# RWKV rounds: modulation sums without a total, a second key buffer, moved exponentials and rates, paired low rank products; a halved forward transform in the Hyena convolutions

## The chip, the cores and the metric

The kernel runs on one core of one Trainium2 chip. The metric is the time of the whole program on the device in microseconds (us). All data are 32-bit floats. Engines: PE is TensorE (matmuls; PEld its weight loads), DVE is VectorE, ACT is ScalarE, POOL is GpSimd, SP is SyncE, whose queue issues most transfers here.

## The reference, cut to what matters

A two-layer block works on 256 latent and 256 context tokens of width 1024. Layer 0 mixes tokens by a bidirectional RWKV-7 recurrence, layer 1 by an order-2 Hyena convolution (latent tokens alone); after each comes a mixture of 32 gated MLPs. The recurrence per head and direction is

```python
sa = jnp.einsum('zbhvk,zbhk->zbhv', S, a_t)
S = S * w_t[..., None, :] + sa[..., None] * b_t[..., None, :] + v_t[..., None] * k_t[..., None, :]
y = jnp.einsum('zbhvk,zbhk->zbhv', S, r_t)
```

with decay, rates and keys made from low rank products (`tanh(x @ w1) @ w2`, `(x @ a1) @ a2`), exponentials and a normalised key `kk`. The modulation rows `cond @ ada_w[i] + ada_b[i]` (6144 columns per layer) scale, shift and gate both layers. Hyena convolves with `irfft(rfft(u) * rfft(kern))`, twice in a row.

## The kernel before, in words

**Stages.** The inputs of the recurrence (to 70 us of the profile), the RWKV heads (71 to 720 us), the experts of layer 0 (from 725 us), the Hyena inputs (1221 to 1355 us), the Hyena convolutions (1356 to 1449 us), the experts of layer 1 (from 1450 us) and a final norm.

**The heads** (`rwkv_heads`) work on one block of 128 channels (two heads) a *round*, eight blocks in all. A round has 24 *slots*, three to a step of the chunked recurrence; here the three slots of a step are called a *hop*, hop 0 (slots 0 to 2) to hop 7 (slots 21 to 23). In round m, four blocks are in work: block m runs its recurrence (`chain`), block m+1 (`now`) has its products and triangular inverse made, block m+2 (`early`) has its projections made, and block m-1 (`behind`) is normalised. Rounds -2 and -1 fill this pipeline.

Each engine has a list of its own, written slot by slot, and runs it strictly in that order; semaphores tie the lists together. The chain of a hop is: PE `chain_state` (L918) → DVE `chain_state` (L1454 or L1456) → PE `chain_solve` (L937, L943) → ACT `chain_solve` (L1187) → PE `chain_close` (L951, L957) → DVE `chain_close` (L1469: the new state H) → next hop. All else is placed between as filler: PE's projections (L775), transposes `turn` (L794), the triangular inverse in levels (`level`, L886: z1, s1, s2, z2, x), products with the values (`from_values_early` L864, `from_values_late` L877, whose halves are called wy0 and wy1), and the feature products (L834 early half, L846 to L852 late half).

**Two rings of banks.** PSUM banks 0 and 1 are shared by all "open" uses in the order of `open_order()`: use i may start only when use i-2 has been read, by ACT or, for names `ys` and `h*`, by DVE. Three more banks serve the inverse in the same way (`inverse_order()`).

**Later modulation** (`LaterModulation`). While the heads run, the rows of `ada_w` that later stages need are multiplied: per round three pieces of 512, 384 and 384 columns, each in two halves (h0 to h5) of four row tiles. `products` (L239) puts the four tiles of a half side by side in four column groups of 32, 512 or 384 columns each; DVE's `modulate` adds the bank to an accumulator (L1490 first half, L1485 second); `total` (L246) sums the 128 partitions with a matmul by ones, ACT copies the row (L1194) and sends it to DRAM. SP loads the weights of h(k) when PE has finished h(k-1).

**Features of block m+1**, on DVE in slots 0 to 5: `key_rates` (L1310), `rates` (L1315), `key_products` (L1320), `features` (L1338 to L1340), `key_sum` (L1327), `features_kr` (L1346, L1348); ACT's `factors` (L1114 to L1118) gives their exponentials in slots 1 and 2. PE's early feature products stand in slot 6.

**Convolutions.** Per order (two) and half of the channels (two): PE transposes, a forward transform of 16 matmul passes (L2648), ACT copies of four banks (L2694), six DVE operations on the spectrum (L2705 to L2712), and 32 passes of the inverse transform (L2657).

## Time and profile before

| what | us |
|---|---|
| three timed runs | 1961.82, 1964.73, 1973.62 (median 1964.73) |
| the profiled execution, own time | 1960.14 |
| its span | 1958.2 |
| rounds 0 to 5 (147.9 to 588.2) | 440.3 |
| round 6, round 7 | 65.1, 52.7 |
| shortest rounds (3 and 4) | 72.0 each |

The page gives busy times over the whole span; since the stages have different limits, the windows by round and by hop say more. A window row has the length of the stretch, then for each engine its busy time and number of instructions, the granted TensorE clock (1.00 is 2.4 GHz, 0.50 is 1.2 GHz), the share of DMA time and GB/s. In a timeline row the bracket is the idle time of the engine before the instruction, and what ended it. A matmul of 32-bit floats shows as two passes.

### The profile page before, as it was taken

Reading aid. Unit: us, or ns where it says so; the run is one execution under the profiler, and the core shown is the slowest. Engines: PE = TensorE matmul, PEld = TensorE weight load, DVE = VectorE, ACT = ScalarE, POOL = GpSimd, SP = SyncE. Lnnn points to the kernel's source line nnn. Section 1 sums busy time; section 2 is a strip of 40 time slices with the busy share of each in tenths; the row PEclk is TensorE's granted clock in tenths of the full one; section 3 lists DMA queues with packets and bytes.
Section 4 is the critical chain, followed back from the end, with each engine's and each line's share of the span. In section 5 each row is a group of like instructions: output and inputs, shape, how many; then the busy total and the mean of one; then the engine's idle time right before and its main releaser. Section 6 shows DMA issues by size and latency. Waiting matters only on the chain. (4 is left out here: it accounts for less than half of the span.)

```text
span 1958.2 us, 34257 instructions
## 1 busy us (share of the span) xinstructions
PE 1776.7 (91%) x13979; PEld 941.9 (48%) x13979; DVE 773.4 (39%) x1910; ACT 531.2 (27%) x993; POOL 52.1 (3%) x45
## 2 busy tenths in 40 slices
PE   5788898898897888999999999898999999999996
PEld 2344555555555544443443443675654444444442
DVE  5766677777777335200100101564735110110101
ACT  3244454554454321111111111213321111111111
POOL 0010000000100000000000001000000000000001
PEclk8989899999999899999999999999999999999998
DMA  9013323323323468999999997232166999999993
GB/s 308 26 33 101 99 73 114 114 77 111 110 76 127 162 238 360 427 428 428 428 429 428 428 416 277 76 128 112 82 272 272 427 428 428 428 428 428 428 413 123
DMA packets 105168, 504.05 MB, mean 257 GB/s; under 512 B 15568, under 2 KB 60352, under 8 KB 79184
## 3 DMA queue, kind: packets, MB, share of 16 engines
q1 hardware_dynamic: 103728, 501.88, 64.4%
q8 instruction: 91, 1.49, 0.3%
q10 hardware_dynamic: 1312, 0.37, 0.1%
q14 instruction: 37, 0.30, 0.0%
HBM read 501.13 MB, written 1.09 MB: 256 GB/s over the span
## 5 line engine op out<-in xcount | busy, mean ns | idle before, releaser
L2009 DVE TENSOR_TENSOR arena<-banks,arena 128x512 f32<-128x512 f32 x32 | 22.1, 692 | 660.5 <-PE banks L1821 660.5
L1821 PE MATMUL banks<-arena 128*64 128x512 f32 x1024 | 226.4, 594 | 10.5 <-DMA arena<-in_moe_w_up 10.5
L1843 PE MATMUL banks<-arena 128*64 128x512 f32 x1024 | 226.8, 596 | 3.3 <-ACT arena L1940 3.3
L1812 PE MATMUL banks<-arena 128*64 128x512 f32 x1024 | 225.3, 593 | 3.3 <-DVE arena L1932 3.3
L775 PE MATMUL banks<-arena 128*128 128x512 f32 (+1 forms) x384 | 159.3, 553 | 0.8 <-ACT arena L1086 0.8
L1821 PEld LDWEIGHTS banks<-arena 128*64 128x64 f32 x1024 | 82.1, 137 | 152.8 <-issue 152.8
L1812 PEld LDWEIGHTS banks<-arena 128*64 128x64 f32 x1024 | 74.2, 137 | 147.8 <-issue 144.2
L1843 PEld LDWEIGHTS banks<-arena 128*64 128x64 f32 x1024 | 70.7, 137 | 154.4 <-issue 150.7
L1934 ACT ACTIVATE arena<-banks,arena 128x128 f32<-128x128 f32 x128 | 48.1, 456 | 335.5 <-PE banks L1801 335.5
L1801 PEld LDWEIGHTS banks<-arena 128*128 128x128 f32 x1024 | 118.4, 194 | 28.1 <-issue 24.3
L1801 PE MATMUL banks<-arena 128*128 128x128 f32 x1024 | 124.5, 281 | 3.5 <-DVE arena L2004 3.5
L1850 PE MATMUL banks<-arena 128*128 128x512 f32 x256 | 115.4, 594 | 2.4 <-ACT arena L1945 2.4
L775 PEld LDWEIGHTS banks<-arena 128*128 128x128 f32 x384 | 69.9, 195 | 59.1 <-issue 50.6
L1944 ACT ACTIVATE arena<-banks 128x512 f32<-128x512 f32 x32 | 19.1, 597 | 282.6 <-PE banks L1843 282.6
L2428 PE MATMUL banks<-arena 128*128 128x256 f32 x384 | 88.9, 391 | 0.0
L2428 PEld LDWEIGHTS banks<-arena 128*128 128x128 f32 x384 | 74.5, 196 | 18.1 <-issue 7.0
L1932 DVE TENSOR_SCALAR arena<-banks,arena 128x128 f32<-128x128 f32 x128 | 43.7, 404 | 97.1 <-PE banks L1801 97.1
L1850 PEld LDWEIGHTS banks<-arena 128*128 128x128 f32 x256 | 46.2, 191 | 50.0 <-issue 45.9
L239 PE MATMUL banks<-arena 128*32 128x384 f32 (+1 forms) x384 | 49.3, 587 | 21.2 <-DMA arena<-in_ada_w 14.1
L1925 ACT ACTIVATE arena<-banks 128x512 f32<-128x512 f32 x32 | 19.1, 597 | 169.7 <-PE banks L1812 169.7
L1187 ACT ACTIVATE arena<-banks 128x128 f32<-128x128 f32 x64 | 17.9, 279 | 133.4 <-PE banks L937 133.4
L918 PE MATMUL banks<-arena 64*64 64x64 f32 x512 | 24.4, 245 | 25.0 <-DVEq L1470 25.0
(394 smaller groups left out, 2398.0 us busy)
## 6 DMA issues: line engine op xcount, KB each, us to landing
arena<-in_moe_w_gate SPq DMA_DIRECT2D x64, 2048.0 KB, 14.9
arena<-in_moe_w_up SPq DMA_DIRECT2D x64, 2048.0 KB, 17.1
arena<-in_moe_w_down SPq DMA_DIRECT2D x64, 2048.0 KB, 12.8
arena<-in_ada_w SPq DMA_DIRECT2D x128, 192.0 KB, 2.9
arena<-in_ada_w SPq DMA_DIRECT2D x64, 256.0 KB, 3.5
arena<-in_rw_wrkv SPq DMA_DIRECT2D x24, 512.0 KB, 5.1
arena<-in_hy_w_in SPq DMA_DIRECT2D x6, 2048.0 KB, 8.4
arena<-in_ada_w SPq DMA_DIRECT2D x8, 1024.0 KB, 17.0
```

The costliest lines, as they stand in the source:

```text
L239: mm = pe.matmul(bank[g * 32:(g + 1) * 32, 0:self.width(piece)], self.cond[:, half * self.HALF + g], self.w[g][:, 0:self.width(piece)], st ...
L775: mm = pe.matmul(s.psum[OPEN.bank(n, name)][:, 0:width], wkv[k][:, t], x[:, t], start=(t == 0), stop=(t == KT - 1))
L918: mm = pe.matmul(s.psum[5 + h][rows(z), 0:C], a_of(par, z, j)[rows(h)], H[rows(h), z], start=True, stop=True)
L1801: mm = pe.matmul((X0, X1)[k // 4][:, k % 4 * P:(k % 4 + 1) * P], hx[:, t, k * P:(k + 1) * P], sel[par][:, t].rearrange("p a b -> p (a b)") ...
L1812: mm = pe.matmul(G[j * CAP:(j + 1) * CAP, :], xT[:, t, j * CAP:(j + 1) * CAP], wg[par][j][:, t], start=(t == 0), stop=(t == KT - 1))
L1821: mm = pe.matmul(U[j * CAP:(j + 1) * CAP, :], xT[:, t, j * CAP:(j + 1) * CAP], wu[j][:, t], start=(t == 0), stop=(t == KT - 1))
L1843: mm = pe.matmul(bank[j * CAP:(j + 1) * CAP, :], hT[:, t, j * CAP:(j + 1) * CAP], wd[j][:, t, half * 512:(half + 1) * 512], start=(t == 0) ...
L1850: pe.matmul(OUT[k][:, :], selwT[par][:, k // 2], y[:, k % 2 * 512:(k % 2 + 1) * 512], start=start, stop=stop).then_inc(scat_done, 1)
L1932: op = eng.tensor_scalar(xT[:, k], src, sc[:, k:k + 1], sh[:, k:k + 1], ALU.mult, ALU.add)
L1934: op = eng.activation(xT[:, k], src, ACT.Identity, bias=sh[:, k:k + 1], scale=sc[:, k:k + 1])
L2009: dve.tensor_tensor(h, U[:, :], sg, ALU.mult).then_inc(h_ready, 1)
L2428: mm = pe.matmul(s.psum[n % 2][:, 0:L], win_ring[k][:, t, q * P:(q + 1) * P], hT[:, t], start=(t == 0), stop=(t == KT - 1))
```

## The change

1. **No totals.** A modulation product now splits its 512 (384) columns over the four column groups, 128 (96) each, and accumulates the four row tiles in the bank: 16 matmuls of 128 (96) columns in place of 4 of 512 (384). DVE adds bias and halves on 128 (96) columns; `total` on PE and on ACT is gone; SP stores the row, in `store`, ahead of the next piece's bias load. The accumulator, bias and row buffers shrink from 512 to 128 columns.
2. **Second key buffer** `KK`; `key_rates`, `key_products` and `rates` of a block move a round ahead, to slots 20, 22 and 23; `inner_factors` (both directions) to slot 21 and `outer_factors(0)` to slot 22 on ACT, `outer_factors(1)` stays in slot 1.
3. **Slots.** Early feature products from slot 6 to 5, h0 from 3 to 2 ahead of wy0, h1 from 6 to 7, `level_two_z` from 7 to 6, `from_values_early` ahead of h3, the decay pair w from 13 to 14 behind h3, the rate pair a behind h4. SP's `load_first` from slot 2 to 4, h1's load from 4 to 3.
4. **Pairs.** `low_rank` takes both banks and issues its two matmuls one after the other; `sum_directions` interleaves its two row halves. ACT evaluates one sigmoid of a constant in slot 11.
5. **Convolutions.** The forward transform multiplies the even and the odd tokens apart (8 passes, no accumulation), and DVE makes the two frequency halves as sum and difference, four operations more; ACT copies the two even banks.

```diff
-        self.acc, self.bias, self.row = s.take(512), s.take(512), s.take(512)
+        self.acc, self.bias, self.row = s.take(P), s.take(P), s.take(P)
...
+    def store(self, sp, m, piece, open_dve):
+        layer, cols = self.place(m, piece)
+        sp.wait_ge(open_dve, OPEN.taken(m, f"h{2 * piece + 1}")[1])
+        sp.dma_start(self.mods[layer, 0, cols].rearrange("(g n) -> g n", g=4),
+                     self.row[0:P:32, 0:self.part(piece)]).then_inc(self.row_out, 16)
...
-        for g in range(self.HALF):
-            mm = pe.matmul(bank[g * 32:(g + 1) * 32, 0:self.width(piece)], self.cond[:, half * self.HALF + g],
-                           self.w[g][:, 0:self.width(piece)], start=True, stop=True, tile_position=(0, g * 32))
+        n = self.part(piece)
+        for t in range(self.HALF):
+            for g in range(4):
+                mm = pe.matmul(bank[g * 32:(g + 1) * 32, 0:n], self.cond[:, half * self.HALF + t],
+                               self.w[t][:, g * n:(g + 1) * n], start=(t == 0), stop=(t == self.HALF - 1), tile_position=(0, g * 32))
...
-        order += [(m, u) for u in ("wy0", "wy1", "h0") if chain]
-        order += [(m, u) for u in ("h1", "t0") if chain]
+        order += [(m, u) for u in ("h0", "wy0", "wy1") if chain]
+        order += [(m, u) for u in ("h1",) if chain]
...
-    BB, KK = [s.take(STEPS, 2, C) for _ in range(2)], s.take(STEPS, 2, C)
+    BB, KK = [s.take(STEPS, 2, C) for _ in range(2)], [s.take(STEPS, 2, C) for _ in range(2)]
...
+                banks = [open_bank(n, f"{name}{z}") for z in range(2)]
+                for z in range(2):
+                    pe.matmul(banks[z][:, :], w[rows(z), :], x[rows(z), :], start=True, stop=True).then_inc(open_done, 1)
...
-                    if now and slot == 1:
-                        factors(n, 0)
...
+                    if early and slot == 21:
+                        inner_factors(q, 0)
+                        inner_factors(q, 1)
+                    if early and slot == 22:
+                        outer_factors(q, 0)
...
-                    if now and slot == 0:
-                        key_rates(n)
+                        features_a(n, 0)
...
                     if early and slot == 20:
                         key_norms(q, 0)
+                        key_rates(q)
...
+                    if early and slot == 22:
+                        key_products(q)
                     if early and slot == 23:
                         unit_keys(q)
+                        rates(q)
...
                         for i in range(TT):
-                            mm = pe.matmul(s.psum[4 + n][:, :], fwd[part][:, i, ft * P:(ft + 1) * P],
-                                           vt[:, i, half * 512:(half + 1) * 512], start=(i == 0), stop=(i == TT - 1))
-                        mm.then_inc(dft_done, 1)
+                            pe.matmul(s.psum[4 + part * 2 + i][:, :], fwd[part][:, i, 0:P],
+                                      vt[:, i, half * 512:(half + 1) * 512], start=True, stop=True).then_inc(dft_done, 1)
...
+                        a, b = half_even[part], s.psum[5 + part * 2][:, :]
+                        dve.tensor_tensor(vhat[:, part, 0, c], a, b, ALU.add)
+                        first, second = ((a, b), (b, a))[part]
+                        dve.tensor_tensor(vhat[:, part, 1, c], first, second, ALU.subtract).then_inc(vhat_ready, 1)
```

How the lists move, at three places. In the rows, "x16" counts equal instructions in a row; the line numbers of the changed kernel differ by a few.

**PE, hop 0's end to the start of hop 2**, before: L886 (64x64 x16) is a level, L877 wy0 and wy1, L918 state, L239 a modulation product, L834 the early feature products.

```order
L886 MATMUL banks<-arena 64x64 x16
L877 MATMUL banks<-arena 64x64 x16
L918 MATMUL banks<-arena 64x64 x4
L877 MATMUL banks<-arena 64x64 x16
L239 MATMUL banks<-arena 32x512 x4
L937 MATMUL banks<-arena 64x64 x4
L943 MATMUL banks<-arena 64x64 x4
L886 MATMUL banks<-x_res,arena 64x64 x16
L886 MATMUL banks<-arena,x_res 64x64 x16
L951 MATMUL banks<-arena 64x64 x4
L918 MATMUL banks<-arena 64x64 x4
```

The same place in the changed kernel (L893 level, L884 wy, L925 state, L253 modulation product, L841 early feature products):

```order
L893 MATMUL banks<-arena 64x64 x16
L253 MATMUL banks<-arena 32x128 x16
L884 MATMUL banks<-arena 64x64 x16
L925 MATMUL banks<-arena 64x64 x4
L884 MATMUL banks<-arena 64x64 x16
L944 MATMUL banks<-arena 64x64 x4
L950 MATMUL banks<-arena 64x64 x4
L893 MATMUL banks<-x_res,arena 64x64 x16
L893 MATMUL banks<-arena,x_res 64x64 x16
L958 MATMUL banks<-arena 64x64 x4
L841 MATMUL banks<-arena 64x64 x32
L925 MATMUL banks<-arena 64x64 x4
```

The product h0 now stands between the level and wy0, and the early feature products between the close of hop 1 and the state of hop 2.

**PE, hop 4's second half and the start of hop 5**, before: L820 ends the rows of block m-1, L766 is the pair w, L951 and L957 close hop 4, L239 is h3, L864 the early values, L918 and L922 the state of hop 5, L246 a total, L775 the key projection.

```order
L820 MATMUL banks<-const,arena 128x128 x2
L766 MATMUL banks<-arena 128x512 x2
L951 MATMUL banks<-arena 64x64 x4
L957 MATMUL banks<-arena 64x64 x4
L239 MATMUL banks<-arena 32x384 x4
L864 MATMUL banks<-arena 64x64 x16
L918 MATMUL banks<-arena 64x64 x4
L922 MATMUL banks<-arena 64x64 x4
L246 MATMUL banks<-arena,const 1x384
L775 MATMUL banks<-arena 128x512 x2
```

Now (L827, L958 and L964, L871, L253, L776, L925 and L929, L785 in the same roles):

```order
L827 MATMUL banks<-const,arena 128x128 x2
L958 MATMUL banks<-arena 64x64 x4
L964 MATMUL banks<-arena 64x64 x4
L871 MATMUL banks<-arena 64x64 x16
L253 MATMUL banks<-arena 32x96 x16
L776 MATMUL banks<-arena 128x512 x2
L925 MATMUL banks<-arena 64x64 x4
L929 MATMUL banks<-arena 64x64 x4
L785 MATMUL banks<-arena 128x512 x2
```

The pair w has moved behind h3 and stands directly ahead of hop 5's state; the total is gone.

**DVE, the end of hop 7 and the start of the next round**, before: L1449 adds the identity to z2, L1475 is the output sum, L1303 the unit keys, L1454 and L1458 the state of hop 0, then key rates (L1310), rates (L1315) and key products (L1320).

```order
L1449 TENSOR_TENSOR x_res<-banks,const 128x512
L1475 TENSOR_TENSOR arena<-banks,arena 128x128
L1303 SCALAR_TENSOR_TENSOR arena<-arena 128x512
L1454 TENSOR_TENSOR arena<-banks,arena 128x2x64
L1458 TENSOR_TENSOR arena<-arena 128x128
L1310 TENSOR_SCALAR arena<-arena 128x1024
L1315 TENSOR_TENSOR arena<-arena 128x8x64
L1315 TENSOR_TENSOR arena<-arena 128x2x4x64
L1320 TENSOR_TENSOR arena<-arena 128x8x64
L1320 TENSOR_TENSOR arena<-arena 128x2x4x64
```

Now (L1446, L1314 key products, L1472, L1296 unit keys, L1308 rates, L1451 and L1455 the state, L1332 the first feature):

```order
L1446 TENSOR_TENSOR x_res<-banks,const 128x512
L1314 TENSOR_TENSOR arena<-arena 128x8x64
L1314 TENSOR_TENSOR arena<-arena 128x2x4x64
L1472 TENSOR_TENSOR arena<-banks,arena 128x128
L1296 SCALAR_TENSOR_TENSOR arena<-arena 128x512
L1308 TENSOR_TENSOR arena<-arena 128x8x64
L1308 TENSOR_TENSOR arena<-arena 128x2x4x64
L1451 TENSOR_TENSOR arena<-banks,arena 128x2x64
L1455 TENSOR_TENSOR arena<-arena 128x128
L1332 SCALAR_TENSOR_TENSOR arena<-arena 128x256
```

The key products and rates now stand ahead of hop 0's state, for the next block but one of the chain; the key rates have moved before these rows, between the two halves of the key norms.

## Rows read from the trace of the kernel before

**Rows 1.** The page: GB/s moved, in 40 slices of 49 us.
```profile
GB/s 308 26 33 101 99 73 114 114 77 111 110 76 127 162 238 360 427 428 428 428 429 428 428 416 277 76 128 112 82 272 272 427 428 428 428 428 428 428 413 123
```

**Rows 2.** Windows: rounds 0 to 5 together, round 6, round 7; columns named first.
```profile
core 0: us, PE busy (x) PEld busy (x) DVE busy (x) ACT busy (x) POOL busy (x), PEclk, DMA share, GB/s
147.90:588.20 440.30, 383.89 (x6133) 237.53 (x6128) 314.32 (x769) 214.75 (x387) 30.09 (x24) 0.97 0.33 98
588.20:653.30 65.10, 51.43 (x979) 34.63 (x978) 42.24 (x110) 28.49 (x54) 4.97 (x4) 0.87 0.42 141
653.30:706.00 52.70, 48.54 (x656) 26.05 (x656) 17.65 (x53) 9.50 (x23) 0.04 (x1) 0.97 0.37 121
```

**Rows 3.** Windows, same columns: the eight hops of round 3.
```profile
370.90:377.90 7.00, 5.55 (x120) 4.78 (x121) 5.29 (x12) 6.11 (x13) 0.00 (x0) 1.00 0.66 175
377.90:385.90 8.00, 4.96 (x151) 3.85 (x147) 6.16 (x15) 3.35 (x7) 0.00 (x0) 1.00 0.41 133
385.90:395.10 9.20, 7.88 (x246) 5.79 (x248) 7.63 (x20) 0.86 (x2) 2.51 (x2) 1.00 0.30 89
395.10:404.50 9.40, 9.40 (x71) 3.91 (x66) 5.93 (x19) 4.15 (x7) 0.00 (x0) 1.00 0.01 3
404.50:413.70 9.20, 7.32 (x115) 4.74 (x111) 7.79 (x20) 5.94 (x11) 0.00 (x0) 1.00 0.49 145
413.70:424.10 10.40, 9.67 (x70) 4.12 (x70) 8.99 (x22) 8.25 (x15) 0.00 (x0) 1.00 0.23 76
424.10:432.00 7.90, 7.90 (x155) 4.91 (x156) 4.41 (x14) 5.29 (x8) 0.00 (x0) 1.00 0.26 80
432.00:442.90 10.90, 9.92 (x138) 6.72 (x133) 6.77 (x9) 2.15 (x6) 2.50 (x2) 1.00 0.36 122
```

**Rows 4.** Timeline of PE, round 3: start, us, line, operation, count, idle before.
```profile
377.10 1.05 PE L877 MATMUL banks<-arena 64*64 64x64 f32 x29 [1.45 <-ACT arena L1081]
...
385.88 0.35 PE L918 MATMUL banks<-arena 64*64 64x64 f32 x8 [2.90 <-DVEq L1470]
...
387.28 1.16 PE L834 MATMUL banks<-arena 64*64 64x64 f32 x64
...
414.87 0.81 PE L246 MATMUL banks<-arena,const 128*1 128x384 f32 x2 [0.73 <-DVE arena L1485]
```

**Rows 5.** Timeline of PEld: the weight loads of one modulation product (eight passes).
```profile
379.43 0.16 PEld L239 LDWEIGHTS banks<-arena 128*32 128x32 f32 x8 [0.27 <-ACT arena L1140]
```

**Rows 6.** Groups of PE: busy us, mean ns, idle before and its releasers.
```profile
L239 PE MATMUL banks<-arena 128*32 128x384 f32 (+1 forms) x384 | 49.3, 587 | 21.2 <-DMA arena<-in_ada_w 14.1 <-ACT arena L1086 6.2
...
L246 PE MATMUL banks<-arena,const 128*1 128x384 f32 (+1 forms) x48 | 22.0, 539 | 4.3 <-DVE arena L1485 4.3
```

**Rows 7.** Timeline of DVE, round 3.
```profile
373.28 1.29 DVE L1315 TENSOR_TENSOR arena<-arena 128x512 f32<-128x512 f32 x2
...
378.82 0.68 DVE L1449 TENSOR_TENSOR x_res<-banks,const 128x512 f32<-128x512 f32 x1
...
394.58 0.28 DVE L1373 TENSOR_TENSOR arena<-banks,const 128x128 f32<-128x128 f32 x1
...
401.96 0.48 DVE L1469 SCALAR_TENSOR_TENSOR arena<-banks,arena 128x64 f32<-128x64 f32 x2 [1.81 <-PE banks L951]
...
413.13 0.47 DVE L1469 SCALAR_TENSOR_TENSOR arena<-banks,arena 128x64 f32<-128x64 f32 x2 [0.18 <-issue]
```

**Rows 8.** Timeline of PE before round 0: the first low rank pair.
```profile
72.80 1.13 PE L766 MATMUL banks<-arena 64*128 64x512 f32 x4 [3.07 <-DVEq L1537]
```

**Rows 9.** Windows, same columns: the stretch right after the same wait in round 0.
```profile
163.00:166.30 3.30, 2.92 (x48) 1.24 (x48) 1.95 (x5) 0.00 (x0) 0.00 (x0) 0.50 0.00 0
```

**Rows 10.** Timeline of the convolutions, PE and DVE.
```profile
1374.97 13.98 PE L2657 MATMUL banks<-arena 128*128 128x256 f32 x64
...
1399.36 7.13 PE L2648 MATMUL banks<-arena 128*128 128x512 f32 x16 [0.79 <-ACT arena L2690]
...
1368.14 1.22 DVE L2706 TENSOR_TENSOR arena<-arena 128x1024 f32<-128x1024 f32 x1
```

More of the change, by code:

```diff
@@ L226, in load @@
             sp.wait_ge(open_done, OPEN.done(*before))
-            if half == 0:
-                sp.wait_ge(open_dve, OPEN.taken(*before)[1])
         if half == 0:
-            sp.dma_start(self.bias[0:1, 0:self.width(piece)], self.ins["ada_b"][layer, cols].unsqueeze(0)).then_inc(self.bias_in, 16)
+            if m or k:
+                self.store(sp, *((m, piece - 1) if piece else (m - 1, self.PIECES - 1)), open_dve)
+            sp.dma_start(self.bias[0:P:32, 0:self.part(piece)],
+                         self.ins["ada_b"][layer, cols].rearrange("(g n) -> g n", g=4)).then_inc(self.bias_in, 16)
         for g in range(self.HALF):
@@ L541, in open_order @@
         order += [(m + 2, u) for u in ("rg",) if early]
-        order += [(m, u) for u in ("t2",) if chain]
     return order
@@ L620, in rwkv_heads @@
     wide = S1b
+    spare = s.take(1)
     later = LaterModulation(s, ins, mods)
@@ L703, in _ @@
                 for slot in range(SLOTS):
-                    if slot == 2 and 0 <= n and n + 1 < CH:
+                    if slot == 4 and 0 <= n and n + 1 < CH:
                         sp.wait_ge(open_done, OPEN.done(n, "rg"))
@@ L807, in sum_directions @@
                 pe.wait_ge(y_ready, HALF * (n + 1))
-                for c in range(HALF):
-                    out = bank[rows(c % 2), c // 2 * P:(c // 2 + 1) * P]
-                    pe.matmul(out, s.c("ident")[:, 0:C], Y[:, c], start=True, stop=False)
-                    mm = pe.matmul(out, s.c("ident")[:, C:P], Y[:, HALF - 1 - c], start=False, stop=True)
+                for pair in range(HALF // 2):
+                    out = [bank[rows(c), pair * P:(pair + 1) * P] for c in range(2)]
+                    for c in range(2):
+                        pe.matmul(out[c], s.c("ident")[:, 0:C], Y[:, 2 * pair + c], start=True, stop=False)
+                    for c in range(2):
+                        mm = pe.matmul(out[c], s.c("ident")[:, C:P], Y[:, HALF - 1 - 2 * pair - c], start=False, stop=True)
                 mm.then_inc(open_done, 1)
@@ L1037, in _ @@
                         modulate(m, 4)
+                    if early and slot == 18:
+                        low_rank(q, "a")
                     if early and slot == 19:
@@ L1054, in _ @@
                         level_two(n, 0)
-                    if chain and slot == 23:
-                        total(m, 2)
                     if m == CH - 1 and slot >= 9:
@@ L1187, in chain_solve @@
                 act.activation(U, s.psum[7][:, 0:P], ACT.Copy).then_inc(us_ready, 1)
-            def total(m, piece):
-                width = later.width(piece)
-                bank = read(m, f"t{piece}")
-                if m or piece:
-                    act.wait_ge(later.row_out, 16 * (later.PIECES * m + piece))
-                act.activation(later.row[0:1, 0:width], bank[0:1, 0:width], ACT.Copy).then_inc(open_act, 1)
-                act.wait_ge(open_act, OPEN.taken(m, f"t{piece}")[1])
-                layer, cols = later.place(m, piece)
-                act.dma_start(mods[layer, 0, cols].unsqueeze(0), later.row[0:1, 0:width]).then_inc(later.row_out, 16)
             for m in ROUNDS:
@@ L1230, in _ @@
                         values(n)
+                    if early and slot == 11:
+                        act.activation(spare, s.c("ones")[:, 0:1], ACT.Sigmoid)
                     if now and slot == 12:
@@ L1237, in _ @@
                         act.activation(outT, read(m - 1, "rows")[:, :], ACT.Copy).then_inc(open_act, 1)
-                    if early and slot == 13:
-                        decay_rank(q, 0)
-                        decay_rank(q, 1)
                     if now and slot == 14:
@@ L1243, in _ @@
                         spread(n)
-                    if chain and slot == 15:
-                        total(m, 1)
+                    if early and slot == 14:
+                        decay_rank(q, 0)
+                        decay_rank(q, 1)
                     if now and slot == 16:
@@ L1261, in _ @@
                         level_two(n, 0)
-                    if chain and slot == 23:
-                        total(m, 2)
-            act.wait_ge(later.row_out, CH * later.PIECES * 16)
         @block.vector
@@ L1574, in _ @@
                         row_scales(m - 1)
-                    if now and slot == 7:
+                    if now and slot == 6:
                         kept_early(n)
@@ L1594, in _ @@
                         modulate(m, 3)
-                    if early and slot == 14:
-                        decay_sum(q, 0)
                     if now and slot == 15:
                         turn_out(n)
+                    if early and slot == 15:
+                        decay_sum(q, 0)
                     if early and slot == 16:
@@ L2614, in hyena_layer @@
         ("vT_done", "vt_ready", "dft_done", "vhat_ready", "real_ready", "imag_ready", "y_done", "y_ready"))
-    o_done, skip_ready = S("o_done"), S("skip_ready")
+    o_done, skip_ready, half_ready = S("o_done"), S("skip_ready"), S("half_ready")
+    half_even = [half_b[:, part] for part in range(2)]
     with nc.Block(name="hyena_convolutions", no_gpsimd_drain=True) as block:
```

148 lines of the change are left out of this document (70 added, 78 removed).

## The prediction

> **What bounds the kernel now.** I first read the page's rate of transfers: about 428 GB/s, level, through the slices of both expert stages [rows 1]. Those stages take weights as fast as they come, and their loads are started by the end of the heads and of the convolutions; so what is won before them shifts them along whole, and only the heads and the convolutions have to be costed. The windows by round come next: rounds 0 to 5 take 440.3 us, 73.4 on average, with PE busy 383.9 of it and DVE 314.3 [rows 2]. PE is nearly the bound, but not quite: in round 3, a round of 72.0 us at full clock throughout, the hops show which engine it is [rows 3]. Hops 3 and 6 are all PE (9.40 of 9.40, 7.90 of 7.90). In hops 1, 2 and 4 PE is idle for 1.3 to 3.0 us. The timeline names the waits: 1.45 us for ACT's transposed values, held up behind the exponentials, and 2.90 us for DVE, which has all features ahead of the new state [rows 4]. In hop 4 it is DVE: from the state of hop 3 (401.96) to that of hop 4 (413.13) it works without a pause of over 0.5 us, 11.2 us, and PE's next state waits for it [rows 7]. So a round alternates between three bounds, and an edit is worth what it does in its own hop.
>
> **The change, hop by hop of round 3.** Prices: 24 totals are busy 22.0 us, 0.92 each, and wait 4.3 us in all for DVE; 48 modulation products take 49.3, 1.03 each [rows 6].
>
> *The new product* is not in the trace. Its 32 passes stream the same number of columns per column group as its 8 passes do now. Sixty-four quadrant passes of 64 columns take 1.16 us [rows 4], so short passes do run abreast. Bounds: 0.8 us (384 columns now) and, if the four groups ran one after another, 32 passes at a quarter of a 512-column pass (7.13 / 16 = 0.446 us [rows 10]), 3.6 us. I take 1.03, unchanged, since the short passes of [rows 4] are the nearest. The weight loads must overlap for that, and now they do: eight loads fall within 0.16 us, under a product still in flight [rows 5].
>
> The Trainium skill, "TensorE: Matmul & The Clock Gate", section "Part 3: Packing small matmuls", says that weight loads overlap matmuls in flight only when the row group differs. All passes of a product share one row group, so by that rule 32 passes would alternate with 32 loads, which is the slow rival below. The eight loads of [rows 5] contradict it, at least for loads to different column groups.
>
> *Hop 0 (7.0):* h0 moves in, 5.55 busy + 1.03 = 6.6, and ACT's hold-up goes, since only one direction's outer exponentials are left between the turned values. wy0's bank now waits for DVE's row means, which come late in the hop: about 0.4. 7.0, no change.
>
> *Hop 1 (8.0):* h0 and the 2.90 us go. A new wait comes: wy1 takes the bank of h0, which DVE reads after its state step and the identity add (0.68 [rows 7]); with the product's add at 128 columns (0.28, as L1373 [rows 7]) and the starts of the two state operations some 0.4, about 1.5 us in which PE has nothing else, since its list is strict. The early feature products (1.0) move in behind the close and need the features, which are now half done by then. 4.96 busy - 1.03 + 1.0 + 1.5 + 0.4 of handing over = 6.8: **-1.2**.
>
> *Hop 2 (9.2):* 7.88 busy - 1.0 (early products) - 0.92 (total) = 6.0; waits for DVE's masking of the banks stay, 0.8: 6.8, **-2.4**.
>
> *Hop 3 (9.4):* all projection: no change.
>
> *Hop 4 (9.2):* here it gets longer. DVE's list is the bound and keeps its length but for one narrower add (0.56 to 0.28), while the pair w, formerly ahead of the close, now stands behind h3 and takes h3's bank. So PE waits for DVE's state (0.47), output sum and product add, about 1.3 us from 413.13 on, then runs the pair (1.13 [rows 8]), and only then hop 5's state, which today starts 0.6 us after 413.13. 1.3 + 1.1 - 0.6 = 1.8, less 0.2 for the add: **+1.6**. Queued behind this wait are the next state and the key projection; PE idles some 2.7 us.
>
> *Hop 5 (10.4):* total and its wait go (0.85 + 0.73 [rows 4]); the key projection waits about 0.3 for ACT's sigmoid, now behind the spread: **-1.2**.
>
> *Hop 6 (7.9):* the pair a waits for h4's add on DVE (0.45) and the norm for the first rate (0.4), less what running side by side saves: **+0.4**.
>
> *Hop 7 (10.9):* the total (0.85) and the wait for weights (9.92 busy of 10.9, part of 14.1 us of such waits over all products [rows 6]) go, as h4 ends earlier; PE waits 0.2 for DVE's state, now behind the key rates: **-1.2**. DVE takes up key rates, products and rates here, 3.4 us (each pair 1.29 [rows 7]); its 4.1 us of idle time in this hop (6.77 busy of 10.9 [rows 3]) covers it. Without that cover the next round's first state would come up to 3.4 us late.
>
> *SP and the rest, at nothing:* the row stores stand ahead of bias and weight loads and wait for DVE's add. For h0 that add comes in the middle of hop 7, some 9 us ahead of the product; for h2 and h4 12 us. h1's weights now precede `load_first`, which is wanted in slot 14. The constant's sigmoid only moves a table load of ACT ahead of the bc and kc copies; the value projection's last part covers it.
>
> Sum: -1.2 - 2.4 + 1.6 - 1.2 + 0.4 - 1.2 = -4.0 per round, 72.0 to 68.0. The six rounds hold 440.3 - 6 × 72.0 = 8.3 us more than six short ones. Most of it is lower clock: right behind the 2.90 us wait the granted clock is 0.50 in round 0 [rows 9], though 1.00 in round 3. The new wait of 2.7 us in hop 4 is of that size, so I keep the 8.3 and count 6 × 4.0 = **24 us**. Round 6 has no block in `early`, so no pair and no +1.6; hops 1 and 2 (3.6), two more totals (1.8) and their waits (0.6): **6 us** of its 65.1. Round 7 has neither features nor pairs: three totals, **2.7 us**.
>
> *Convolutions.* The forward transform falls from 7.13 us to half, four times: 14.3 us of PE's work [rows 10]. DVE gets four operations on a bank per half, 0.68 each as the add of the same shape in [rows 7], beside six of 1.22 [rows 10] and their drains: 11 us a half. DVE then bounds both halves: one order is 1.04 + 0.74 + 1.8 (transposes, copy, first two banks) + 22 + 3.5 (a quarter of the 13.98 us inverse) = 29.1 us, against 1.04 + 0.74 + 7.13 + 1.04 + 0.79 + 7.13 + 13.98 = 31.9 now. Two orders: **5.7 us**, between nothing and 14.3.
>
> In all 24 + 6 + 2.7 + 5.7 = 38.4, so 1960.1 becomes 1921.7. That is the profiled execution; the median of the timed runs lies 4.6 above it and the fastest 1.7. I forecast **1924** for the new median, 2.1% below 1964.7. About 1% (19.6 us) is what a measurement of this kernel tells from no change.
>
> **The rivals.**
>
> A, the forecast: 1910 to 1938 as single terms vary, chance 0.52.
>
> B, *DVE's lists take over*. PE now meets DVE at wy1 and at the pair w in every round. If both waits come out 0.5 longer, and the clock is at its lower level for 3.3 us behind each hop 4 (1.65 us lost), 4.0 becomes 1.3 per round: 8 + 4 + 2.7 + 3 = 18 us, 1944. For it: DVE is busy 53 of 72 us and idles little in hops 4 and 5. Against: hop 5 has slack on PE. Chance 0.24.
>
> C, *more than counted*: lower clock gone and the wait in hop 4 half covered, 6.5 us per round: 39 + 6 + 2.7 + 5.7 = 53, 1909. Chance 0.14.
>
> D, *slower*: the narrow passes don't run abreast. A product then costs 3.6 in place of 1.03 at 128 columns and 1.9 more at 96; a round 2 × 2.5 + 4 × 1.9 = 12.6 us more, eight rounds 101: 2025. It decides from 1.2 us a product on (38 + 20 over 48). [Rows 4] and [rows 5] speak against it. Chance 0.04.
>
> E, *the edits don't bite*: the pairs run one after the other (+0.9 each, 11 us in six rounds) and the convolutions are held by DVE at today's length (5.7): 1941. [Rows 8] shows a pair abreast when both banks are free. Chance 0.06.
>
> **How the numbers follow.** The time is A's. Below 1945 lie A, C, most of E and half of B: faster 0.82; same, the rest of B and E, 0.13; slower, D and a little of the unforeseen, 0.05. The range 1906 to 1946 leaves out D, the upper end of B and the lower of C, 0.18 in all.
>
> **What would show it.** Windows by hop should show hops 1 and 2 at about 6.8 each, hop 4 near 10.8 with an idle time of PE of about 2.7 ended by DVE's add ahead of the pair, no wait of the state of hop 2, and a product group still near 1.03 us each. A product at 2 us or more makes D; a hop 5 at lower clock in most rounds makes B. The convolutions should take 88 us with PE waiting for DVE in the inverse. Hop 4 no longer than now would make the +1.6 wrong; rounds above 71 us, the whole ledger.

## The result and the profile after

On one chip, in alternation, the kernel before took 1965.83 us and the changed one 1946.5 (medians of seven runs each): a ratio of 0.9902, 95% interval [0.9879, 0.9925]. The kernel became faster by 1%, not by the forecast 2.1%. The profiled executions differ by less than the medians: the span falls from 1958.2 to 1944.6, 13.6 us where the ledger has 38.4.

Windows of the changed kernel for rounds 0 to 5, round 6 and the part of round 7 that answers to [rows 2]; columns: stretch, length, busy time (instructions) of each engine, granted clock, DMA share, GB/s.

```profile
core 0: us, PE busy (x) PEld busy (x) DVE busy (x) ACT busy (x) POOL busy (x), PEclk, DMA share, GB/s
153.60:583.30 429.70, 368.18 (x6958) 256.11 (x6956) 307.37 (x770) 206.10 (x375) 30.03 (x24) 0.95 0.33 99
583.30:645.90 62.60, 46.64 (x1122) 37.51 (x1119) 38.47 (x108) 23.78 (x45) 4.00 (x4) 0.89 0.45 147
645.90:695.70 49.80, 44.98 (x806) 28.08 (x802) 15.82 (x53) 7.96 (x19) 1.04 (x1) 1.00 0.43 139
```

Six rounds win 10.6 us, not 24. PE has 15.7 us less to be busy with than in [rows 2], at a mean clock of 0.95 (0.97 before). Round 6 wins 2.5 (forecast 6), round 7 2.9 (2.7). And the chain starts 5.7 us later, at 153.6 in place of 147.9: the fill rounds, for which the ledger has no term. These four make 10.3 us; the other 3.3 are won behind the heads, 2.1 of them in the two orders of the convolutions (64.4 to 62.4). The expert stages are level at 428 GB/s as in [rows 1], so all that is won ahead of them counts.

The eight hops of round 4, which is typical (72.0 us), in the same columns; they answer to [rows 3].

```profile
439.20:447.00 7.80, 6.65 (x162) 5.63 (x158) 6.27 (x16) 3.59 (x8) 0.00 (x0) 1.00 0.35 109
447.00:454.80 7.80, 6.19 (x202) 6.05 (x200) 4.07 (x11) 2.56 (x5) 0.00 (x0) 0.78 0.93 286
454.80:463.10 8.30, 5.94 (x221) 5.35 (x212) 5.14 (x15) 0.28 (x1) 2.51 (x2) 1.00 0.17 46
463.10:472.60 9.50, 9.50 (x93) 4.50 (x89) 7.01 (x24) 4.19 (x7) 0.00 (x0) 1.00 0.19 55
472.60:483.80 11.20, 6.99 (x138) 4.97 (x134) 7.95 (x21) 7.25 (x14) 0.00 (x0) 0.98 0.39 119
483.80:494.10 10.30, 10.17 (x65) 4.63 (x64) 8.24 (x20) 6.74 (x11) 0.00 (x0) 0.86 0.25 77
494.10:502.00 7.90, 7.02 (x182) 5.13 (x183) 4.60 (x15) 5.09 (x8) 0.00 (x0) 1.00 0.33 104
502.00:511.30 9.30, 8.98 (x158) 6.93 (x156) 8.65 (x11) 5.00 (x10) 2.49 (x2) 1.00 0.16 49
```

Hops 3, 6 and 7 are within 0.1 of the forecast or better. Hops 1 and 5 have a granted clock of 0.78 and 0.86: each holds a stretch at 0.50, and the clock column says where the time went before any wait is looked at. PE's waits in the same round, the longest ones (total, times, longest):

```profile
PE banks L776 <- DVE arena L1484: 3.5, 1, 3.5
PE banks L884 <- DVE arena L1487: 1.6, 1, 1.6
PE banks L893 <- issue: 1.5, 1, 1.5
PE banks L853 <- DVE arena L1370: 0.8, 1, 0.8
PE banks L944 <- DVE arena L1451: 0.7, 1, 0.7
```

The first two are the waits that the forecast introduced: the pair w (L776) behind DVE's add of h3, 3.5 where 2.7 was reckoned, and wy1 (L884) behind the add of h0, 1.6 where 1.5 was. The third has no releaser: PE pauses in the middle of a level whose first passes have run. Nothing like it stands in rounds 0 to 5 before; here there are 7.2 us of it in six rounds. Right behind the two waits, two windows:

```profile
449.20:452.60 3.40, 3.40 (x70) 3.40 (x72) 2.03 (x5) 0.77 (x2) 0.00 (x0) 0.50 0.93 289
483.30:486.70 3.40, 3.27 (x21) 1.56 (x20) 2.02 (x5) 1.27 (x2) 0.00 (x0) 0.50 0.51 150
```

Both are full of work, as in [rows 9], at half the clock (the 1.2 GHz level). Stretches of this kind hold 44.4 us of rounds 0 to 5, 23.9 before; at the pair w one begins in each of the six rounds (in two of them up to 0.9 us before the wait ends), behind wy1 in five.

Why the pair waits so long stands in DVE's list (timeline; start, us, line, operation, idle before):

```profile
477.00 1.03 DVE L1425 TENSOR_TENSOR x_res<-arena 128x512 f32<-128x512 f32 x1
478.11 0.69 DVE L1427 TENSOR_REDUCE arena<-x_res 128x64 f32<-128x512 f32 x1
478.87 1.07 DVE L1431 TENSOR_TENSOR x_res<-arena 128x512 f32<-128x512 f32 x1
480.01 0.69 DVE L1433 TENSOR_REDUCE arena<-x_res 128x64 f32<-128x512 f32 x1
480.88 0.48 DVE L1466 SCALAR_TENSOR_TENSOR arena<-banks,arena 128x64 f32<-128x64 f32 x2 [0.19 <-issue]
481.48 0.29 DVE L1472 TENSOR_TENSOR arena<-banks,arena 128x128 f32<-128x128 f32 x1
482.11 0.26 DVE L1484 TENSOR_TENSOR arena<-banks,arena 128x96 f32<-128x96 f32 x1 [0.34 <-issue]
```

PE ended h3 at 478.99. DVE is in the largest step of its triangular solve until 480.70, and only then come the close and the add (L1484) that frees the bank.

The products themselves, all rounds; 1536 rows of the new kind:

```profile
L253 PE MATMUL banks<-arena 128*32 128x96 f32 (+1 forms) x1536 | 46.5, 260 | 8.8 <-DMA arena<-in_ada_w 7.1
```

46.5 / 48 = 0.97 each, in place of 1.03 in [rows 6], with 7.1 us of waits for weights in place of 14.1. The rows of PE in the convolutions' two orders:

```profile
1347.10 5.26 PE L2646 MATMUL banks<-arena 128*128 128x512 f32 x8 [0.69 <-ACT arena L2687]
...
1368.27 10.07 PE L2654 MATMUL banks<-arena 128*128 128x256 f32 x32 [3.25 <-DVE arena L2713]
...
1385.27 3.70 PE L2646 MATMUL banks<-arena 128*128 128x512 f32 x8 [0.74 <-ACT arena L2687]
1388.87 7.45 PE L2654 MATMUL banks<-arena 128*128 128x256 f32 x32
1399.56 7.45 PE L2654 MATMUL banks<-arena 128*128 128x256 f32 x32 [3.24 <-DVE arena L2713]
```

The transform takes 3.70 where it took 7.13 [rows 10], and DVE then holds the inverse up by 3.24. The second order, at full clock, lasts 28.7 us (1378.18 to 1406.85); before it was 31.4. In the first order the same rows take 5.26 and 10.07, at half clock for part of them: 33.7.

### The profile page after: what moved, and what is told of

It is laid out like the page before. It is cut to its first block and busy times, and to the rows that moved or that the text cites. A ratio compares the mean times of both kernels' runs of the same rounds, so it can differ in the third digit from the quotient of the medians.

```text
span 1944.6 us, 36382 instructions
## 1 busy us (share of the span) xinstructions
PE 1745.5 (90%) x15051; PEld 963.6 (50%) x15051; DVE 772.1 (40%) x1926; ACT 515.4 (27%) x969; POOL 52.1 (3%) x45
## 5 line engine op out<-in xcount | busy, mean ns | idle before, releaser
L785 PE MATMUL banks<-arena 128*128 128x512 f32 (+1 forms) x384 | 166.4, 572 | 2.7 <-ACT arena L1086 2.4
L785 PEld LDWEIGHTS banks<-arena 128*128 128x128 f32 x384 | 72.4, 202 | 60.9 <-issue 47.3
L253 PE MATMUL banks<-arena 128*32 128x96 f32 (+1 forms) x1536 | 46.5, 260 | 8.8 <-DMA arena<-in_ada_w 7.1
L1466 DVE SCALAR_TENSOR_TENSOR arena<-banks,arena 128x64 f32<-128x64 f32 x112 | 26.8, 280 | 65.1 <-PE banks L958 61.9
L776 PE MATMUL banks<-arena 64*128 64x512 f32 x64 | 22.5, 777 | 27.0 <-DVE arena L1484 18.6
## 6 DMA issues: line engine op xcount, KB each, us to landing
arena<-in_moe_w_up SPq DMA_DIRECT2D x64, 2048.0 KB, 17.1
```

The lines of the kernel that those rows point to most:

```text
L253: mm = pe.matmul(bank[g * 32:(g + 1) * 32, 0:n], self.cond[:, half * self.HALF + t], self.w[t][:, g * n:(g + 1) * n], start=(t == 0), stop ...
L776: pe.matmul(banks[z][:, :], w[rows(z), :], x[rows(z), :], start=True, stop=True).then_inc(open_done, 1)
L785: mm = pe.matmul(s.psum[OPEN.bank(n, name)][:, 0:width], wkv[k][:, t], x[:, t], start=(t == 0), stop=(t == KT - 1))
L1466: dve.scalar_tensor_tensor(H[:, z], s.psum[5 + z][:, 2 * C:3 * C], fade[m % 2][:, z, j:j + 1], Hf[:, z], ALU.mult, ALU.add)
```

## The experiments

Ratios are to the kernel before, in runs on the same chip; 0.001 is 2 us. Variants are compared with one another by these ratios. Figures for rounds and hops come from one profiled execution of each; two executions with unchanged heads (before, and the convolutions alone) take 440.3 and 441.3 for rounds 0 to 5.

### One wait away at a time

The pair w back ahead of the close (lists of PE and ACT, and the ring of banks):

```diff
+                    if early and slot == 13:
+                        low_rank(q, "w")
...
-                    if early and slot == 14:
-                        low_rank(q, "w")
```

> The changed kernel with the pair w back where it was, ahead of the close of hop 4 and of h3 (ACT's sigmoids of it ahead of its spread, as before). Theory CLOCK: the 3.5 us wait and the low clock behind it go; hops 4 and 5 together fall from 21.5 to about 18.5 where PE stays fed, fill rounds get about 3 us shorter: about 1926. Theory WAITS: DVE's state is what hop 5 waits for whichever way, so hop 4 stays at 10.3 or more, PE waits about 2.5 us for the state in place of the pair, and the low clock stays behind that: 1938 to 1944, most of the gain in the fill rounds.

0.9803, [0.9783, 0.9823]; median 1929.14. Windows for rounds 0 to 5 and for hops 4 and 5 of round 4:

```profile
154.60:568.10 413.50, 360.20 (x6964) 254.69 (x6961) 306.79 (x770) 205.91 (x375) 30.02 (x24) 0.97 0.35 103
464.70:473.50 8.80, 7.02 (x136) 5.02 (x132) 7.41 (x19) 6.53 (x13) 0.00 (x0) 1.00 0.49 151
473.50:482.40 8.90, 8.88 (x68) 4.01 (x68) 7.29 (x20) 7.43 (x13) 0.00 (x0) 1.00 0.28 90
```

21.5 us have become 17.7, and the clock is 1.00: the wait for DVE's close is now covered by the pair, and no stretch at 0.50 stands at hop 4 in any round. This is CLOCK's picture; only the fill rounds did not get shorter (first state at 154.6). Over the six rounds hops 4 and 5 win 4.2 us on average, of which hops 2 and 6 give back 1.6; the pauses without a releaser grow from 7.2 to 10.2 us in all.

h0 behind wy1 again:

```diff
-        order += [(m, u) for u in ("h0", "wy0", "wy1") if chain]
+        order += [(m, u) for u in ("wy0", "wy1", "h0") if chain]
```

> The changed kernel with h0 back behind wy0 and wy1, so that wy1 no longer takes the bank that DVE reads late. Theory CLOCK: the wait of 1.6 us and the low clock in hop 1 go; hops 0 to 2 fall from 23.4 to about 20.5 in rounds 1 to 6: 1946.5 - 6 x 2.7 = about 1930. Theory WAITS: DVE's features set the early products, and PE waits in hop 1 or 2 for those; hops 0 to 2 stay above 22.5: 1941 to 1947.

0.9832, [0.9816, 0.9848]; median 1932.75. Hops 0 to 2 of round 4:

```profile
430.40:436.50 6.10, 5.40 (x130) 4.71 (x128) 5.58 (x14) 3.59 (x8) 0.00 (x0) 1.00 0.33 107
436.50:443.20 6.70, 6.04 (x236) 5.50 (x235) 4.72 (x14) 2.67 (x5) 0.00 (x0) 1.00 0.35 101
443.20:450.60 7.40, 5.74 (x219) 5.33 (x210) 5.17 (x15) 0.28 (x1) 2.52 (x2) 1.00 0.80 228
```

23.9 has become 20.2, with no stretch at 0.50 in hop 1, while those behind the pair w stay. So in these runs each wait keeps its own low stretches: taking one away leaves those of the other. Rounds 0 to 5 take 415.4. Not all of that is wait and clock: the pauses without a releaser nearly go too, 1.6 us in the six rounds in place of 7.2.

Both together:

> The changed kernel with both: the pair w ahead of the close of hop 4 and h0 behind wy1. Alone they took 17.4 and 13.8 us off 1946.5 (rounds 0 to 5: 413.5 and 415.4 in place of 429.7). If the two waits are independent, as the forecast's ledger by hops has it: rounds 0 to 5 near 400, 1946.5 - 31 = about 1915. If DVE's list is the next bound (it is busy about 53 us of a round), PE waits for DVE elsewhere and less than 24 of the 31 come: above 1922.

0.9754, [0.9731, 0.9778]; median 1917.35. Below the changed kernel (0.9902) that is 9.9 and 7.0 thousandths alone and 14.8 together, 29 us of a sum of 33: the waits are nearly independent.

### The wait kept, the clock kept up

Multiplications of the identity, whose result nobody reads, in front of the two waiting operations:

```diff
+                        s.keep_warm(pe, inverse_bank(m, "s1l"), 3)
                         from_values_late(m, 1)
...
+                            s.keep_warm(pe, inverse_bank(n, "z1c"), 7)
                         low_rank(q, "w")
```

> The changed kernel (1946.5) with TensorE kept busy in its two new waits: three multiplications of the identity with constants (512 columns, 0.43 us each as the four at the end of the convolutions) ahead of wy1, seven ahead of the pair w, into a bank that the inverse takes next. The waits for DVE stay as long as they are. Theory CLOCK (the clock that falls to 0.50 behind these waits costs most of what is missing; rounds 0 to 5 hold 44 us of such stretches, 20 before, on 42 us of PE work): the stretches behind the two waits go, hops 1 and 5 get about 1.5 shorter each, rounds 0 to 5 fall from 429.7 to about 414, the kernel to about 1930. Theory WAITS (DVE's list sets the end of hops 1, 2, 4 and 5, and a faster PE only waits longer): the stretches go but rounds 0 to 5 stay above 425 and the kernel above 1941.

0.9952, [0.9934, 0.997], slower than the changed kernel: neither theory's number. The amount was wrong. The timeline of PE in hop 4 of round 4:

```profile
486.90 6.28 PE L94 MATMUL banks<-const 128*128 128x512 f32 x14
493.11 1.13 PE L776 MATMUL banks<-arena 64*128 64x512 f32 x4
```

Seven multiplications are 14 passes and end 4 us after the bank was free. With one and three of them:

> The changed kernel with TensorE kept busy in its two new waits, by the right amount this time: a multiplication of 512 columns is two passes of 0.43, 0.87 us (14 rows in 6.3 us in the run with seven), so one ahead of wy1 (wait 1.6) and three ahead of the pair w (2.6 of 3.1 to 3.6 us). Theory CLOCK: the stretches at 0.50 behind both waits go and nothing else gets longer; hop 5 falls from 10.6 to 9.4 and hop 1 by 0.5 as in the run with too much work, rounds 0 to 5 from 429.7 to about 418, the kernel to about 1934. Theory WAITS: no gain, 1943 or more.

0.987, [0.9849, 0.9891]; median 1936.65. Rounds 0 to 5 take 423.0 in place of 429.7, and 17.1 us of them are at 0.50 in place of 44.4, all behind pauses (below), none behind the two waits. The clock alone, with the waits as they were, is worth 6.7 us there and about 6 in the ratio. The two intervals overlap, so the timed runs alone do not settle it; the windows speak for it, and the run with few passes below, which fills the waits in the same way, takes 420.6. Hops 1 and 5 of round 5 (9.4, with a pause of 1.4 in it, and 10.1 in the changed kernel):

```profile
513.20:519.40 6.20, 5.64 (x204) 4.75 (x201) 4.06 (x11) 2.56 (x5) 0.00 (x0) 1.00 0.90 279
548.40:557.80 9.40, 8.99 (x70) 4.03 (x68) 7.97 (x20) 6.72 (x11) 0.00 (x0) 1.00 0.28 86
```

CLOCK's expectation for these two hops came true, but part went back in hop 2: the pauses without releaser grew from 7.2 to 11.2 us over six rounds. So 6.7 is what is left after that.

### Is it the order of DVE's list?

```diff
+                    if chain and slot == 14:
+                        modulate(m, 3)
                     if now and slot == 14:
                         base_level(8, wide)
                         dve.sem_inc(base_ready, 1)
```

> The changed kernel with DVE's close of hop 4 and h3's add ahead of the 8-wide base solve (3.7 us of DVE's list, 477.0 to 480.7 in round 4), which then lies under the pair w and the key projection. Theory ORDER (the pair's wait is neither ACT's nor the bank order's, but 3.7 us of DVE work that stands in front of it in DVE's list): the wait falls from 3.5 to below 0.8, the low clock behind it goes, hops 4 and 5 fall from 21.5 to about 18, rounds 0 to 5 by 15 to 20 us: about 1929. Theory WAITS (DVE's list is the bound whatever its order): the solve of hop 5 or the first level of hop 6 then waits for DVE by as much, hops 4 to 6 stay at 29 or more: 1942 to 1948.

0.9987, [0.9971, 1.0004]: slower than the changed kernel by 8.5 thousandths, 17 us. The pair's wait fell to 0.5, but PE's key projection then waited for ACT's reading of the pair, which stood behind a spread that waited for DVE (PE, then ACT):

```profile
488.36 3.78 PE L785 MATMUL banks<-arena 128*128 128x512 f32 x4 [5.03 <-ACT arena L1086]
```

```profile
485.32 2.14 ACT L1173 ACTIVATE x_res<-arena,const 128x256 f32<-128x256 f32 x4 [4.21 <-DVEq L1434]
487.62 1.27 ACT L1086 ACTIVATE arena<-banks,arena 128x512 f32<-128x512 f32 x2 [0.16 <-issue]
```

With ACT's list mended too (the pair's sigmoids ahead of the spread):

> The changed kernel with DVE's close of hop 4 and h3's add ahead of the 8-wide base solve, as in the run that came out 15 us slower, and on ACT the pair w's sigmoids now ahead of the spread (there the spread stood first, waited for the later solve, and PE waited 5.0 us behind it for the pair's bank). Theory ORDER (the pair's 3.5 us wait is DVE's 3.7 us of base solve in front of it, and the slower run failed by ACT's list alone): the wait is below 0.8, no wait of 5 us comes, hops 4 and 5 fall from 21.5 to about 18, the kernel to about 1930 as with the pair put back. Theory WAITS (DVE's and ACT's lists are the bound): hops 4 to 6 stay at 29 or more, 1942 or more.

0.9896, [0.9878, 0.9914]: no better than the changed kernel (0.9902). Hops 4 to 6 of round 4:

```profile
468.30:476.40 8.10, 6.89 (x144) 5.02 (x136) 5.71 (x19) 5.13 (x10) 0.00 (x0) 1.00 0.55 164
476.40:488.00 11.60, 9.09 (x70) 4.01 (x68) 9.00 (x21) 9.07 (x16) 0.00 (x0) 1.00 0.22 69
488.00:498.40 10.40, 9.74 (x179) 6.28 (x182) 6.10 (x18) 4.95 (x8) 0.00 (x0) 0.67 0.25 79
```

ORDER fell: 30.1 us for the three hops, 29.4 in the changed kernel. What hop 4 won, hops 5 and 6 gave back, with a new wait of 1.96 for DVE ahead of the state and a low stretch behind it. The lists read as a chain of their own, solve, ACT's spread, transposes and the inverse's first level: DVE now waits 1.53 us for the spread ahead of the transposes, and the state of hop 6 waits for DVE. Delaying the head of that chain delays its end. So neither order of DVE's list that was tried cures the pair's wait; giving PE something that needs no DVE does, which is what the old place of the pair did.

### The pauses without a releaser

Each product in 8 rows of the full width, as before the change, in place of 32, on the kernel that is kept busy by the right amount:

```diff
-            for g in range(4):
-                mm = pe.matmul(bank[g * 32:(g + 1) * 32, 0:n], ...
+            mm = pe.matmul(bank[t * 32:(t + 1) * 32, 0:4 * n], ...
```

> The kernel with TensorE kept busy in both waits by the right amount (1936.65), and each new product in 4 multiplications of the full width in place of 16 of a quarter: 8 rows of 512 or 384 columns, abreast as before the change, in place of 32. It leaves out the sum over the four partial products, so DVE adds one of four parts; TensorE's time for a product stays near 1.0. Theory SUPPLY (PE's instructions do not come fast enough where hops 1 and 2 are dense with short passes: pauses of 1.4 to 2.2 us that the profile puts down to no release stand there in every round, 12.5 us in rounds 0 to 6 of that kernel, 0.6 before the change): with 24 passes fewer in each product the pauses fall below 4 us in all, hop 2 from 10.4 to about 8, the kernel to about 1927. Theory OTHER (the pauses come from somewhere else, the number of passes does not matter): pauses as before, 1933 to 1940.

0.9861, [0.9829, 0.9893]; median 1939.79. The pauses stay: 11.5 us in rounds 0 to 5. One in hop 2 of round 2, and the products' group:

```profile
308.19 0.63 PE L840 MATMUL banks<-arena 64*64 64x64 f32 x27 [2.13 <-issue]
```

```profile
L252 PE MATMUL banks<-arena 128*32 128x384 f32 (+1 forms) x384 | 47.2, 565 | 4.9 <-DMA arena<-in_ada_w 4.9
```

SUPPLY fell as far as the number of the products' passes goes: PE has 6146 passes in these rounds, 6958 in the changed kernel, and 6133 before the change, with no pause.

The trace does show what the pauses end with. Queue q8 moves instructions in transfers of 16 KB, and their number goes with PE's: 55 in rounds 0 to 5 of the changed kernel for 13.9 thousand rows of PE and its weight loads, 49 before for 12.2 thousand, about 250 rows each. All six pauses of this run that last 0.5 us or more end 1.32 to 1.47 us after such a transfer has landed; the one at 308.19 follows a landing at 306.82. In ten profiles of the changed kernel and its variants it is 51 of 51, at 1.27 to 1.60 us, where a transfer comes only every 8 us or so. So PE most likely waits for its own instructions there. That is argued from times: no run changes how they are brought, and why they come late in these places stays open.

The group's row settles a term: wide and narrow passes cost the same, 0.98 and 0.97 a product.

### The convolutions

> The kernel before with the new convolutions alone. The undisturbed second order of the changed kernel takes 28.7 us (31.4 before): 2.7 each, 5.4 for two, against 5.7 in the forecast. If the low clock at the convolutions' start and after the 3.2 us wait of the first inverse comes again, as in the changed kernel's profile, half of that or less: 2 us. So 0.999 to 0.997 of the kernel before.

0.9996, [0.9977, 1.0015]: no difference. The forecast 5.7 us (0.9971) lie outside, the 2 us that the expectation allows with a low clock inside. In its profile the two orders take 31.5 and 30.1 us, 33.1 and 31.4 before: in both, the second half of the inverse comes at 0.50 for 3.4 us behind the 3.24 us wait. Filling that wait, on the best kernel:

> The kernel with the pair w and h0 back and the rates late (1914.9), and three multiplications of 512 columns (2.6 us) in the 3.24 us that PE waits for DVE in each inverse of the convolutions. In the run of the convolutions alone the inverse's second half took 8.56 and 8.86 us at the lower clock behind that wait, 7.45 at full. If these stretches take back the convolutions' gain: 2 x 1.2 = 2.4 us at most, about 1912.5. If not: 1914 to 1917.

0.9742, [0.9717, 0.9766], against 0.9744 without: no difference that can be told.

### The fill rounds, and the rest

> The changed kernel without the constant's sigmoid that loads ACT's table ahead of the bc copies. From the first pair w to the first state of the chain the profiles show 75.1 and 76.4 us with the old order, 79.4 to 79.8 with the new. If the table load there (1.28 us, PE's wait for the copies 1.34) is what the fill rounds lost: 78 or less. If it is DVE's earlier key products or the pair's place: 79 or more.

> The changed kernel with DVE's key rates, rates and key products back in hop 0 of the next round. If these 3.4 us of DVE's work, which in the fill round stand in front of the first state, are what the fill rounds lost: 76 to 78 us from the first pair w to the first state, in place of 79.4 to 79.8, and the features of hops 0 to 2 come late in each round. If not: 79 or more.

From the first pair w to the first state these two profiles show 78.5 and 79.6 us, where the changed kernel has 79.6. So DVE's earlier products explain nothing of it, and the table load 1.1 at most. Not even that much is shown: a variant that keeps the load (all_moves, below) has 78.2. What goes with these times is the clock. The kernel before, then the changed one, over this stretch:

```profile
72.80:147.86 75.06, 57.62 (x455) 33.04 (x456) 46.99 (x97) 31.55 (x52) 4.99 (x4) 0.84 0.13 39
74.00:153.60 79.60, 58.48 (x453) 33.60 (x456) 48.22 (x100) 34.89 (x59) 5.01 (x4) 0.79 0.12 37
```

At 0.50 are 23.9 us of it before (75.1), 26.6 in the run with the convolutions alone (76.3), 30.7 without the sigmoid (78.5) and 33.8 in the changed kernel and with the keys back (79.6). No run fills the waits of these rounds, so that the clock is the cause is likely and not shown.

Over the whole kernel the two edits cost time, in one run each: 1959.95 without the sigmoid, where the table load comes behind the pair w in each of the six rounds and hop 5 takes 13.0 on average; 1956.88 with the keys back, where hop 0 takes 9.9. So these two parts of the change look worth having.

> As the kernel with both edits, and DVE's rates (two products, 1.29 us) behind the state of hop 0 in place of ahead of it, where PE's solve of hop 0 waits 0.7 us for DVE. If that wait is on the path: about 0.7 less in each of the six rounds, 4 us. If DVE's list only shifts (the features come 1.29 later either way): within 2 us of the kernel with both edits.

0.9744, [0.9721, 0.9767]; median 1914.88. Hop 0 is 0.4 shorter and hop 1 0.6 longer: DVE's list only shifts. It is level with both edits alone, 2.6% below the kernel before; no version is better by more than the noise. Rounds 0 to 5:

```profile
152.80:553.80 401.00, 355.62 (x6962) 249.12 (x6960) 306.67 (x770) 205.81 (x375) 30.07 (x24) 0.99 0.36 106
```

Moving h1 into hop 3, and that with the filled waits of the convolutions, gave 0.9753 [0.9723, 0.9783] and 0.9757 [0.9731, 0.9783]: nothing more.

> The kernel with the pair w and h0 back and the rates late (1914.9), and h1 moved from hop 2 (slot 7) to the start of hop 3 (slot 9), which is all wide projection. Theory SUPPLY: the pauses of 1.0 to 2.4 us in hops 1 and 2 of that kernel get about 0.7 us shorter per round, hop 3 gets the product's 1.08 that hop 2 loses: 1909 to 1912. Theory OTHER: the product is only moved, 1913 to 1917.

> The kernel with the pair w and h0 back, the rates late, h1 at the start of hop 3 and TensorE kept busy in the convolutions' waits: the sum of the two runs beside it, about 1908 if both give what SUPPLY and the clock say, 1914 if neither does.

## Why the prediction was wrong

The direction was right and the size was not: the span is 24.8 us short of the ledger's 38.4. The six rounds lack 13.4, the fill rounds 5.7, the convolutions 3.6 and round 6 3.5; 1.4 came unforeseen. Step by step:

- **The new product**, costed at 1.03: 0.97. Right, and with it [rows 4] and [rows 5] against the slow rival. By the rule of the Trainium skill, "TensorE: Matmul & The Clock Gate", section "Part 3: Packing small matmuls", 32 passes to one row group would have alternated with their loads; the trace disagrees, since 8 wide and 32 narrow rows cost the same (0.98 and 0.97).
- **Hop 0** (7.0): 7.5 on average over the six rounds, 7.6 in most. PE's solve waits 0.7 for DVE, whose rates now stand in front of the state; hop 7's entry reckoned 0.2 for that.
- **Hop 1** (6.8): 8.0. The wait for h0's bank was foreseen, at 1.5 (1.61). Not foreseen was the clock: five of the six rounds have a stretch at 0.50 behind it. Filled, the hop takes 6.7.
- **Hop 2** (6.8): 7.5. The 2.90 us are gone; pauses that no row before shows came instead.
- **Hop 4** (10.8) and **hop 5** (9.2): 11.3 and 10.6. The pair's wait is 2.2 to 3.6, 3.1 on average (18.6 in six), in place of 2.7, and hop 5 begins at half clock each time. With the wait filled hop 5 takes 9.3.
- **Hops 6 and 7** (8.3 and 9.7): 7.9 and 9.4, better than forecast.
- **Round 6** (6): 2.5. Hop 1 holds one pause of 2.84 us, most of what is missing.
- **Fill rounds** (0): 5.7 later, 1.2 of it before the first pair w. Two profiles with the old heads need 75.1 and 76.3 from there to the first state, the changed kernel 79.6, with more of it at half clock. I costed the edits for a full round alone; a fill round has no chain to lie under.
- **Convolutions** (5.7): an order at full clock gains 2.7 (forecast 2.85), but the wait that the change puts into the inverse takes the clock with it in three of the four orders that the changed kernel and the run with the convolutions alone show, and the gain cannot be measured.

The step that failed is the sentence that closes the ledger: "The new wait of 2.7 us in hop 4 is of that size, so I keep the 8.3". It gave six rounds with *two* new waits the low clock of six rounds with one old one: 23.9 us at 0.50 became 44.4. [Rows 9] had shown what stands behind such a wait. Kept busy, the same kernel is 6.7 us shorter in those rounds; the pauses, which the ledger lacks as well, hold another 7.2. Together that is about the 13.4 us that the six rounds are short of the forecast. No run shows this split by itself: filling the waits lengthened the pauses by 4.0, and other hops miss up and down. Rival B named the mechanism, low clock behind each hop 4, and its 1944 is close to what came. That is in part luck: its own terms, 8 + 4 + 2.7 + 3, stand against 10.6, 2.5, 2.9 and 2.1, and it has neither the low clock behind wy1 nor the pauses nor the loss in the fill rounds. Its chance of 0.24 was too low, since nothing in the trace spoke against it but two rounds (3 and 4) in which the old wait had left the clock at 1.00.

What the change was reckoned to free is there once both waits are taken out by the old order of two operations: the kernel then stands at 1917 and 1915. For the six rounds the ledger gives 416.3; less its own price of the two waits (1.5 and 1.6 a round) that is 397.7, and the profile shows 399.3. This holds for the sum more than for the hops: hop 2 takes 9.1 there.

## What to carry to other kernels

A wait of PE costs its length and, in many rounds, half speed on the dense work behind it. When an edit makes PE wait anew, price it as a range: from the wait alone up to the wait and one stretch at half clock, as long as the low stretches of that trace last, once per wait. Before moving an operation behind another engine's late step, ask what PE could do in that wait that needs no one; the operation that was moved away may have been it. And cost an edit once more for the rounds that fill a pipeline, where nothing covers it.

## What the hardware showed beyond the forecast

- The clock fell to 0.50 within 2 us of the end of the wait at wy1 (1.61 us) in 5 of 6 rounds, and at the pair w (2.2 to 3.6 us) in 6 of 6. The 2.90 us wait before the change had it in 5 of 7 rounds of one execution and 6 of 7 of another, with the heads unchanged. So a round without it in one execution promises nothing for the next.
- The length of a wait does not decide it alone. The same 1.61 us at wy1 had a low stretch behind it in 4 of 6 rounds with the pair put back, in 1 with DVE's close first, and in none with ACT's list mended too. The 1.45 us that PE waited for ACT in hop 0 before the change had none in rounds 1 to 6.
- In the rounds the low stretches last 3.41, 6.83 or 10.24 us. Useless work in the wait kept the clock at 1.00; too much of it (6.28 us where the bank was free after 2.2) cost more than it gave.
- PE paused, mostly for 1.4 to 2.2 us, inside dense rows of short passes, with no releaser, in the changed kernel and its variants (1.6 to 12.1 us in rounds 0 to 5), and in no round 0 to 5 of the kernel before. Each pause of 0.5 us or more ended 1.27 to 1.60 us after a 16 KB transfer of instructions had landed.
